# Split weight operands kept in DRAM and operand sums moved to VectorE in the mixers of a streaming encoder

## The reference, cut to what matters

```python
z = rmsnorm(x, norm1) @ w_in
bg, cg, h, q, k, v, gr, r = jnp.split(z, SPLITS, axis=-1)
cv, conv_new = causal_dwconv(cg * h, conv_prev, conv_w)
y_conv = rmsnorm(bg * cv, g_conv)
logg = jax.nn.log_sigmoid(gr @ w_alpha + b_alpha) / GATE_TAU
o, gla_new = gla(q, k, v, logg, gla_prev)      # chunks of 64, a recurrent state per head
y_gla = rmsnorm(o, g_gla) * jax.nn.silu(r)
x = x + jnp.concatenate([y_conv, y_gla], -1) @ w_out
u = rmsnorm(x, norm2) @ w_up                   # 2 * 2816 columns
x = x + (silu(conv(g)) * conv(a)) @ w_down     # a, g: halves of u
y = rmsnorm(x, final_norm)
```

## Time and profile before

| | us |
|---|---|
| median of 3 runs (lowest, highest) | 2481.1 (2477.91, 2482.54) |
| the profiled execution, its own time | 2475.78 |
| its span, first to last instruction | 2473.7 |

### The profile page before, as it was taken

How to read it: one execution, slowest core, us unless ns; L and a number is a source line. 1 busy time by engine, 2 the same in 40 slices (tenths; PEclk the granted TensorE clock), 3 DMA queues, 4 the chain that set the end, 5 groups by cost and what they waited for, 6 DMA issues and landing times. The chain is left out here.

```text
span 2473.7 us, 39507 instructions
## 1 busy us (share of the span) xinstructions
PE 2292.7 (93%) x12602; PEld 2087.3 (84%) x12602; DVE 1817.0 (73%) x2655; ACT 1046.9 (42%) x2037; POOL 1386.6 (56%) x1459
## 2 busy tenths in 40 slices
PE   7899887999887888799999999999999998999997
PEld 5788775988766877689999998899999997999996
DVE  6467866377774577679888988766766778887876
ACT  4444452444353444534444444533333336443434
POOL 6655625645527556477787777444444445555552
PEclk9899998999998999999999999999999999999999
DMA  3112433212442125644444446744444456555553
GB/s 118 52 52 60 145 111 115 69 44 63 151 150 71 52 60 192 246 171 158 173 146 166 163 160 231 254 151 145 155 141 160 145 175 230 191 195 191 195 191 104
DMA packets 257555, 355.04 MB, mean 144 GB/s; under 512 B 12188, under 2 KB 195313, under 8 KB 257457
## 3 DMA queue, kind: packets, MB, share of 16 engines
q1 hardware_dynamic: 257457, 353.77, 42.7%
HBM read 276.54 MB, written 77.19 MB: 143 GB/s over the span
## 5 line engine op out<-in xcount | busy, mean ns | idle before, releaser
L1543 PE MATMUL ps<-xo,wq 128*128 128x384 f32 (+1 forms) x1848 | 599.7, 325 | 24.8 <-DVE r L2400 5.4
L1544 PE MATMUL ps<-xo,wq 128*128 128x384 f32 (+1 forms) x1848 | 598.5, 324 | 0.0
L1545 PE MATMUL ps<-xo,wq 128*128 128x384 f32 (+1 forms) x1848 | 598.3, 324 | 0.0
L2333 DVE TENSOR_TENSOR resid<-resid,ps 128x512 f32<-128x512 f32 (+1 forms) x728 | 477.6, 681 | 75.3 <-PE ps L1545 45.9
L961 POOL TENSOR_TENSOR wq<-wu_raw,wq 128x256 fp32r<-128x256 f32 x396 | 379.2, 980 | 108.3 <-ACT wq L1073 108.3
L1543 PEld LDWEIGHTS ps<-xo,wq 128*128 128x128 f32 x1848 | 350.4, 190 | 47.6 <-issue 25.4
L1544 PEld LDWEIGHTS ps<-xo,wq 128*128 128x128 f32 x1848 | 351.2, 190 | 20.3
L1545 PEld LDWEIGHTS ps<-xo,wq 128*128 128x128 f32 x1848 | 351.3, 190 | 0.0
L494 POOL TENSOR_TENSOR wq<-wu_sum,wq 128x256 fp32r<-128x256 f32 x240 | 200.8, 860 | 223.1 <-ACT wq L1193 223.1
L2350 DVE SCALAR_TENSOR_TENSOR up_y<-up_u,params,up_y 128x768 f32<-128x768 f32 (+1 forms) x264 | 286.8, 1086 | 49.0 <-ACT up_y L1117 30.7
L1543 PE MATMUL ps<-wd_hi,hid_hi 128*128 128x512 f32 x704 | 277.1, 394 | 8.4 <-DVE resid L2333 8.4
(11 more groups left out here) (246 smaller groups left out, 4598.4 us busy)
## 6 DMA issues: line engine op xcount, KB each, us to landing
wq<-w_ops SPq DMA_DIRECT2D x176, 512.0 KB, 4.5
wu_raw<-in_w_up_dram SPq DMA_DIRECT2D x89, 512.0 KB, 4.2
w_ops<-wq SPq DMA_DIRECT2D x88, 512.0 KB, 2.7
wd_raw<-in_w_down_dram SPq DMA_DIRECT2D x66, 512.0 KB, 5.3
wu_raw<-in_w_in_dram SPq DMA_DIRECT2D x60, 512.0 KB, 3.9
x_in<-in_x_prompt_dram SPq DMA_DIRECT2D x32, 512.0 KB, 5.0
raw<-in_w_out_dram SPq DMA_DIRECT2D x24, 512.0 KB, 4.0
wu_raw<-in_w_up_dram SPq DMA_DIRECT2D x43, 256.0 KB, 3.1
```

The lines of the kernel that those rows point to most:

```text
L1543: pe.matmul(out, lh, rh, start=(first and n == 0), stop=False, skip_group_check=skip)
L1544: pe.matmul(out, ll, rh, start=False, stop=False, skip_group_check=skip)
L1545: last = pe.matmul(out, lh, rl, start=False, stop=end, skip_group_check=skip)
L2333: last = dve.tensor_tensor(resid[0:m, t, s], resid[0:m, t, s], ps[0:m, bank, :], ALU.add)
```

## The change

Seven edits:

1. In block one SP stores the split operands 1, 3, 4, 6 of every pair to DRAM (`m_ops`); in blocks two and three it loads them into `wq`. There DVE makes no weight sums, ACT and POOL split only 0, 2, 5, and of the second source part only one quarter is loaded.
2. x operand 4 is made by DVE in two steps (5 and 6) in place of POOL's three; operand 5 takes two steps (7 and 8) in place of three and no longer waits for the gate products. All nine steps stand together, ahead of the low parts.
3. ACT reads the fifth value tile before it makes the high parts of x operands 1 and 3, and the sixth before that of 4.
4. In pairs one to three of block one (p = 1, 2, 3) DVE makes the low parts of weight operands 2 and 4.
5. ACT's and DVE's weight work sits later: the sums after product 4 (before: 3), the high parts one product later each.
6. The gate steps of the first tile come earlier, the first outputs two products later, six products are left for the end (before five), so that fewer stand between the GLA steps. `conv_norm` stands after the second tile of pass 1 (before: after the last tile of pass 0).
7. Between blocks ACT makes the high parts of the last two value units before the last x tile's.

The core of the diff (index arithmetic of semaphores left out):

```diff
-AT_GATE, AT_SUMS, AT_SCORES = (1, 6), (3, 1), (4, 2)
-LEFT = 5
-LOW_PAIRS, LOW_OPS = (), ()
+AT_GATE, AT_SUMS, AT_SCORES = (0, 6), (1, 5), (4, 2)
+LEFT = 6
+SCORES_TO_OUTPUTS = 2
+LOW_PAIRS, LOW_OPS = (1, 2, 3), (2, 4)
...
-def low_by_v(p, i):
-    return p in LOW_PAIRS and i in LOW_OPS
...
             products = [(p, i) for p in range(NPAIR) for i in range(NP)]
             steps = [(s, t) for t in range(TILES[b]) for s in ("XYZ" if tile_cols(b, t)[1] == P else "XZ")]
-            out, g = [], products.index(AT_SCORES) + 1
+            out, g = [], products.index(AT_SCORES) + 1 + SCORES_TO_OUTPUTS
             for p, i in products[:g]:
                 out.append(("G", p, i))
                 if (p, i) in (AT_GATE, AT_SUMS, AT_SCORES):
...
             def load_pair(b, p, part):
                 n = (A11, A21)[part]
-                sp.dma_start(wu_raw[:, n:n + 2, :].rearrange("p n (k c) -> p (n k) c", c=P),
-                             pair_source(p, part)).then_inc(mix_sems[f"w_loaded{part}"], 16)
+                if b and part:
+                    sp.dma_start(wu_raw[:, A22, :].rearrange("p (k c) -> p k c", c=P),
+                                 pair_source(p, part)[:, 4:8]).then_inc(mix_sems[f"w_loaded{part}"], 16)
+                else:
+                    sp.dma_start(wu_raw[:, n:n + 2, :].rearrange("p n (k c) -> p (n k) c", c=P),
+                                 pair_source(p, part)).then_inc(mix_sems[f"w_loaded{part}"], 16)
+            def store_pair_op(p, i):
+                pair_split(sp, p, i)
+                sp.dma_start(m_ops[p, KEPT.index(i)], wq[:, WQ_AT[i]].bitcast(F32)).then_inc(op_stored[KEPT.index(i)], 16)
+            def load_pair_op(b, p, i):
+                if p:
+                    mixes[b].wait(sp, "p_done", NP * (p - 1) + i + 1)
+                else:
+                    mixes[b].wait(sp, "v_done", TILES[b])
+                sp.wait_ge(op_stored[KEPT.index(i)], 16 * NPAIR)
+                sp.dma_start(wq[:, WQ_AT[i]].bitcast(F32), m_ops[p, KEPT.index(i)]).then_inc(op_loaded[KEPT.index(i)], 16)
...
                 for p in range(NPAIR):
                     for part in range(2):
+                        if b == 0 and p:
+                            for i in ((1,), (3, 4))[part]:
+                                store_pair_op(p - 1, i)
                         if p:
                             pair_split(sp, NPAIR * b + p - 1, (2, 5)[part])
                         load_pair(b, p, part)
+                    if b == 0 and p:
+                        store_pair_op(p - 1, 6)
+                    if b:
+                        for i in KEPT:
+                            load_pair_op(b, p, i)
...
                 for n, i in enumerate((2, 5, 5, 6)):
+                    for k in {0: (1,), 1: (3, 4), 3: (6,)}.get(n, ()) if b == 0 else ():
+                        store_pair_op(NPAIR - 1, k)
                     pair_split(sp, NPAIR * b + NPAIR - 1, i)
                     load_unit(sp, out_unit(b, n))
...
-                n1.wait(pool, "lo", 2 * nt)
-                wait(pool, sums_stored, 16 * 4 * b)
-                if b == NB - 1:
-                    pool.wait_ge(gap_zero, 4)
-                c = HALF[b]
-                t1 = unsplit(b, 4)
-                for step, (left, left_part, right, right_part, op) in enumerate([
-                        (xt_hi, c, xt_hi, 0, ALU.subtract), (None, 0, xt_lo, c, ALU.add), (None, 0, xt_lo, 0, ALU.subtract)]):
-                    mix.wait(pool, "t1_step", step)
-                    for k in range(4):
-                        a = left[:, k, left_part:left_part + c].bitcast(F32) if left else t1[:, k]
-                        last = pool.tensor_tensor(t1[:, k], a, right[:, k, right_part:right_part + c].bitcast(F32), op)
-                    mix.inc(last, "t1_step")
                 for p in range(NPAIR):
-                    for i in range(NP):
-                        if not low_by_v(p, i):
+                    for i in SPLIT[b]:
+                        if not low_by_v(b, p, i):
                             pair_low(pool, NPAIR * b + p, i, pair_low_p, 2)
...
+                    mix.wait(act, "t_step", {1: 5, 3: 5, 4: 7, 5: 9}[i])
...
                 def high_pair(s, i):
                     p = s % NPAIR
+                    if i not in SPLIT[b]:
+                        return
                     if i in A_RAW:
                         mix.wait(act, "w_loaded1" if i == 5 else "w_loaded0", 16 * (p + 1))
-                        if i:
+                        if i and b == 0:
                             mix.wait(act, "w_summed", 4 * p + 4)
                     else:
                         mix.wait(act, "w_summed", 4 * p + SUM_ORDER.index(A_SUM[i]) + 1)
+                    if i in KEPT:
+                        wait(act, op_stored[KEPT.index(i)], 16 * p)
                     mix.inc(act.activation(wq[:, WQ_AT[i], 0], wu_source(i), ACT.Copy), "w_hi")
...
                 for n in range(nt - 4 if b == 0 else 0, nt):
                     read_values(n)
-                    if n == 3:
+                    if n == 4:
                         high_sum(1)
                         high_sum(3)
-                    if n == 4:
-                        high_sum(4)
...
                     high_pair(NPAIR * b, 2 + n)
+                    if n == 0:
+                        high_sum(4)
                 high_sum(5)
                 high_pair(NPAIR * b, 4)
                 high_pair(NPAIR * b, 5)
...
                     kind, u = PAIRS[p]
                     done = NP * p + i + 1
                     if i == 0:
-                        mix.wait(act, "p_done", NP * p)
-                        high_pair(s, 6)
                         mix.wait(act, "p_done", done)
                         mix.wait(act, "c21_read", p)
...
+                        if p:
+                            high_pair(s, 5)
+                    if i == 1:
+                        high_pair(s, 6)
...
                     if p + 1 < NPAIR:
-                        for n in {1: (0,), 4: (1, 2), 5: (3,), 6: (4, 5)}.get(i, ()):
+                        for n in {2: (0,), 5: (1, 2), 6: (3, 4)}.get(i, ()):
                             mix.wait(act, "p_done", NP * p + n + 1)
                             high_pair(s + 1, n)
...
-                    if nxt and 1 <= j <= TILES[nxt]:
-                        first_high(nxt, j - 1)
                     if j == nt and nxt:
                         for slot in (2, 3):
                             high_unit(act, v_unit(nxt, slot), (mix, "out_done", 8 * nt))
+                    if nxt and 1 <= j <= TILES[nxt]:
+                        first_high(nxt, j - 1)
...
                     bank = {0: 0, 2: 0, 4: 2, 6: 2}.get(i, 1)
-                    pair_split(pe, s, i)
+                    if i in SPLIT[b]:
+                        pair_split(pe, s, i)
+                    else:
+                        pe.wait_ge(op_loaded[KEPT.index(i)], 16 * (NPAIR * (b - 1) + p + 1))
...
-                t_raw, t2_raw = unsplit(b, 3), unsplit(b, 1)
+                t_raw, t2_raw, t1_raw, n4 = (unsplit(b, i) for i in (3, 1, 4, 5))
                 operand_step(0, 3, b22, b12[0], ALU.subtract)
                 operand_step(1, 3, t_raw, b22_l, ALU.add)
                 operand_step(2, 3, t_raw, b12[1], ALU.subtract)
                 operand_step(3, 1, t_raw, b11, ALU.add)
                 operand_step(4, 1, t2_raw, b11_l, ALU.add)
-                pair_sums(0)
+                if b == 0:
+                    pair_sums(0)
+                wait(dve, sums_stored, 16 * 4 * b)
+                operand_step(5, 4, b22, t2_raw, ALU.subtract)
+                operand_step(6, 4, t1_raw, b22_l, ALU.add)
+                operand_step(7, 5, b21, t2_raw, ALU.subtract)
+                operand_step(8, 5, n4, b21_l, ALU.add)
                 operand_low(1, 1)
                 operand_low(2, 3)
                 operand_low(3, 4)
                 mix.wait(dve, "v_done", nt)
                 mix.wait(dve, "g_done", nch)
-                mix.wait(dve, "t_lo", 3)
-                t2, n4_raw = high_low(1), unsplit(b, 5)
-                operand_step(5, 5, b21, t2[0], ALU.subtract)
-                operand_step(6, 5, n4_raw, b21_l, ALU.add)
-                operand_step(7, 5, n4_raw, t2[1], ALU.subtract)
                 operand_low(4, 5)
                 mix.wait(dve, "zeros", 3)
...
                     if i == 3:
                         mix.wait(dve, "p_done", done)
                         mix.inc(dve.tensor_tensor(r_3m[:, 0:c], ps[:, 1, 0:c], r_1[:, 0:c], ALU.add), "r3_read")
-                        if p + 1 < NPAIR:
-                            pair_sums(p + 1)
                         if kind == "bg":
                             conv_taps(u, 1)
                     if i == 4:
                         mix.wait(dve, "p_done", done)
                         mix.wait(dve, "r3_read", p + 1)
                         pair_quarter(p, 1, 1, 2, r_3m, "c22_read")
```

(11 more changed lines are left out.)

48 lines of the change are left out of this document (27 added, 21 removed).

## The result

The changed kernel takes 2419.6 us (median of 4 runs, 2412.3 to 2428.1) against 2480.7 before: ratio 0.9756, 95% interval 0.9722 to 0.9789. The gain is 61 us in the medians and 54.5 in the profiled spans (2473.7 to 2419.2). I had forecast 40.5, 2441 us, so the direction was right and the size short by 21 us; 2419.6 lies at the very end of my range of 2420 to 2460.

The account below looks back on a forecast made before the run. PE was taken as the bound, with some 134 us idle in the mixers, where the order of DVE's and POOL's work counts. Terms 52 + 2.5 - 19 + 5 = 40.5 us off 2481.1 gave 2441 us, range 2420 to 2460.

Parts of the forecast that it names:

- Starts: Starts of blocks one, two and three: first four products done earlier, gains of 15, 20 and 17 us, together 52.
- DVE now decides: Start of block one: DVE's steps, sums and low parts end with `r_2` at 68.6, so product (0,3) ends near 71.
- Between the blocks: Between blocks one and two: about half of PE's 4.68 us wait for value unit 2 goes, gain 2.5 us.
- The output projection: Start of pass 2, each block: later `conv_norm` delays POOL's low parts; PE waits 4.4 us plus 2 slow, loss 19 us.
- The rival without a chain: Output projection: no chain behind `conv_norm`, as POOL catches up or ACT's copies overlap; 19 us more gain, 2422 us; chance 0.12.
- Between the products: Pairs of all blocks: relief of DVE, ACT and POOL against short GLA steps, net gain 5 us, bounds -6 and +10.
- I take 8, bounds 3 and 10: Pairs of block three: less work on DVE frees PE from `conv_u` and `qk` waits of 8.1 us; gain 8 us.
- the wait at 778.49: Block three: PE's 4.34 us wait for a quarter behind the next pair's sums goes, with 2 us of low clock.
- The dealt-out steps: GLA steps with one product between them cost 4 us in block one, 2 in two; 2 and 1 come back.
- The third rival: Starts: DVE and POOL lock each other out, DVE instructions take 2.5 us, ends 6, 3 and 1 us later; 2451; chance 0.10.
- The loads: Pairs with kept operands: no PE wait for `op_loaded` expected; the rival had late, slower loads cost 140 us, 2581; chance 0.04.

Follow-up runs that it names:

- experiments 4 and 5: Changed kernel with POOL making x operand 4 again: 2442.2 us; with ACT's high parts of operands 1, 3, 4 ahead of value reads: 2418.0; with both: 2448.9.
- experiment 2: Changed kernel without kept weight operands in the mixers (all sources loaded, four sums, seven operands split, none stored): 2466.9 us, ratio 0.9949.
- experiment 6: Changed kernel with the old deal-out of the GLA steps and five last products: 2415.9 us, ratio 0.9745.

## Why the prediction fell short

**Starts, right in size.** 14.5 us against 15 in block one, 16.4 against 16.2 in the stretch to block two; block three's stretch gained 2.1 against 4.7, within its scatter. In block one the last 2 us were POOL's and not DVE's: the step "DVE now decides" was wrong there, by a rival's mechanism in the other direction (below), and that the sum still came out is luck. That POOL's operand 4 held the start is shown by experiments 4 and 5, with one correction: I had put the gain on ACT's read of value six ahead of the operand, and that order alone is worth nothing. At block three's start operand 4 returns 3.8 us and the kept operands 10.0 (experiment 2), where I had named DVE's four steps and four low parts. Of block one's 14.5 us these two edits return 6.2 when undone; the other 8 I put on operand 5, which DVE no longer makes behind the gate products. That was not tried by itself.

**Between the blocks, right for the wait.** 2.5 forecast; the wait fell by 2.9. I charged no clock to it, and undoing it brought that back as well, some 5 us in the medians, which is not clear of their scatter.

**The output projection, right.** 19 forecast, 20 measured by taking it back, with the waits and the low clock as forecast. The rival without a chain gave 2422, near the time measured, but its mechanism is refuted: the loss is there, and was covered by more gain elsewhere.

**Between the products, the step that failed.** The term "I take 8, bounds 3 and 10" for block three, and -2 for block two. Measured were 30.5 in block three (with 6.3 more for the wait at 778.49 and its clock, 14.3 forecast) and 5.3 in block two; together 23.5 us over the forecast, where the whole was short by 14 in the profiled execution and 21 in the medians. Two errors lie in it. The larger is the clock: I charged it to the waits of the starts and of pass 2, and 2 us here, but 13.6 us of the 30.5 are PE's own busy time. The smaller is the idle: I priced the relief by the rows `conv_u`, `qk` and the one `gla_y` wait of 4.34, 12.3 us, and not by PE's whole idle in these pairs, 23.0 us, of which 16.9 went; the k_end and `gla_y` (L2100) waits hang on the same chain, and come back with it (experiment 2). Not all of the 30.5 is the kept operands': they give 27.8 back when undone, and the deal-out 6.4, which overlap. The kept operands are the larger part of the change, 47 of 61 us, and I had priced them at 8 between the products, 14 with the wait at 778.49 and its clock.

**The dealt-out steps, right for block one.** -4 forecast, -5.7 measured, 5.3 of which come back. Block two's -2 was -3.4 (experiment 6), and the kept operands give 5.4 there (experiment 2); the stretch gained 5.3, and the 3.3 us that the two leave open no run assigns. That the same deal-out gives 6.4 us in block three I didn't foresee.

**DVE and POOL at the starts.** The third rival had DVE's instructions at 2.5 us. They took 1.76 alone and 1.96 to 2.29 beside POOL. It was POOL that paid: 0.73 us for an instruction alone, up to 2.25 beside DVE's x instructions. The Trainium skill, SBUF — State Buffer, Who interferes with whom, calls it an exclusive lock. The trace agrees that the two slow each other, and shows POOL's instruction at about three times its time alone and DVE's at 1.1 to 1.3 times; how the two are arbitrated no row shows.

**The loads.** No wait of PE for `op_loaded` in any kernel with kept operands, as forecast. The stores, which I had counted only as bandwidth, made sources late by their place in the queue; with the sums' later place PE felt little of it.

## What to carry to other kernels

When an edit takes work from several engines, bound it by all of PE's idle time in the stretch plus the busy time that PE loses to low clock (here 23.0 us and, measured afterwards, 13.6; from the row of before, (1 - 0.94) x 175 = 10.5 us would have been an estimate), not by the waits whose names match the edit: a chain of four engines shows under whatever name stands last. The kept operands gave the block with the shortest tiles most in its pairs, 27.8 us against 5.4: they take away weight work that doesn't shrink with the tile. And a deal-out or an order that is best for one block may be worst for another: here a constant for each block and a chain started one pass earlier were worth 29 us more than the change.

## Not expected of the hardware

A POOL instruction of 128x256 took 0.73 us alone and up to 2.25 beside DVE's 128x1536 instructions, which slowed from 1.76 to between 1.96 and 2.29 only. The same products of block three kept PE busy for 152.0 us at a mean granted clock of 0.94 and for 138.4 us at 0.99.
